# Nine load buffers, and an end that keeps the residual in PSUM, in a mixture-of-experts layer

## The chip, the cores and the metric

The kernel runs on one core of a Trainium2 chip. The metric is the device time of one execution in microseconds (us). The engines are TensorE (PE in the profile), VectorE (DVE), ScalarE (ACT), GpSimd (POOL) and SyncE (SP). SP issues nearly all transfers (DMA); they are carried out by 16 DMA engines. SBUF is the working memory and PSUM the memory that TensorE writes.

## The reference, cut to what matters

One layer of a causal decoder trunk on 256 tokens of 1024 channels, all in float32. It has an RMS norm, an input projection, a pooling mixer and a dilated attention, an output projection added to the residual, and then a mixture of experts, again with an RMS norm, and a last norm:

```
x = x + concat(y_pool, y_attn) @ w_out
t = rmsnorm(x, g_ffn)
logits = t @ w_router + b_router            # 32 experts
top 4 per token, softmax over the four      # combine[token, expert]
for e in range(32):
    gu = t @ w_gu[e] + b_gu[e]              # 1024 x 2048
    gate = min(gu[:, :1024], 7);  lin = clip(gu[:, 1024:], -7, 7)
    act = gate * sigmoid(1.702 * gate) * (lin + 1)
    out += combine[:, e] * (act @ w_down[e] + b_down[e])    # 1024 x 1024
result = rmsnorm(x + out, g_final)
```

Each expert's weights are 8 MB for gate and up and 4 MB for down, so the 32 experts are 402 million bytes that have to be read.

## The kernel before, in words

**Stages.** Up to about 100 us of the profile the kernel runs norm, projections, attention and router. From there it works through the experts, two at a time: a pair is one iteration, and there are 16 pairs. (If an expert has more than 64 tokens the whole set of pairs is run again for the tokens left over; how often is computed on the chip into `further`. For these inputs it is zero.)

**One pair.** Each expert takes up to 64 tokens (`SLOTS`). The tokens of both experts are gathered by matrix products with a 0/1 matrix (`disp`, built by DVE) into xT. For an expert TensorE multiplies xT with gate and up weights (`gu_unit`, eight chunks), ScalarE copies the sum to `gu`, TensorE turns it (`turn_gu`, line 1142), DVE adds the biases (line 840) and clips, ScalarE takes the sigmoid, DVE forms actT, and TensorE multiplies it with the down weights (`down_unit`). ScalarE copies that into ysc. In the next pair TensorE spreads it back to the tokens (`scatter`, two halves of tokens with two halves of columns each) and DVE adds it to the residual acc (line 857). Expert a's down product and gate and up product of the next pair's first expert overlap with the element-wise work of the other one.

**The load buffers.** Weights come in units of 2 MB: four for gate and up, two for down of each expert, 12 for a pair, 192 in all. There are RAW = 8 buffers of 16 KB on each partition. TensorE waits for `raw_loaded` of a buffer, and after the last product with it raises `unit_used`. SP waits for `unit_used` to reach a load's number less RAW, and issues the load (line 322, waiting at 354). SP's queue is worked through in order, whatever an item waits for.

**Before the first pair** SP issues four units of expert 0 and four of expert 1 as soon as their places in SBUF are free, among them b_down into ysc[:, 0] (line 335, after a memset by POOL at line 407), b_gu (line 340) and g_final (gfin, line 342). TensorE runs the gate and up product of expert 0 (line 1155), turns the combine weights (line 1158, `comb_turned`), turns the gate and up biases, 16 transposes (line 1166, `bias_turned`), and starts on the pairs. The first pair has a scatter too: it scatters b_down, weighted with the combine weights that lie in dispT[:, 0].

**The loop** holds two pairs, since 24 units are three times round the eight buffers; the last two pairs are written out behind it.

**The end.** After the last but one unit's product TensorE scatters the pair's first expert (`last_scatter(0)`), then comes the last unit, ScalarE and DVE copy half of its result each (lines 574 and 891), and `last_scatter(1)` adds it. DVE adds the four pieces to acc (line 896). ScalarE squares and sums the rows of each tile of 128 tokens (line 581), DVE takes mean and reciprocal (lines 722 and 723), ScalarE the root (584). POOL multiplies tile 0 with gfin (line 417), DVE tile 1 (line 900), ScalarE and DVE scale one tile each (587, 903), and SP stores them (373).

## Time and profile before

| what | value |
|---|---|
| median of 3 runs | 1038.89 us (1037.91 to 1041.66) |
| the profiled execution | 1037.48 us, its span 1034.8 us |
| PE busy | 956.8 us (92%) |
| DVE, ACT, POOL busy | 28%, 13%, 2% |
| transfers | 419.41 MB, mean 405 GB/s |
| largest groups of transfers | 128 of w_gu and 64 of w_down, 2048 KB each |
| granted clock of TensorE | 0.996 |

The span is from the first to the last instruction of the profiled execution, and the execution's time is 2.7 us more. Engine shares are of the span. In the profile a float32 product of TensorE shows as two MATMUL records and a transpose as one. A row of a timeline that ends with x8 merges eight records. "L909" is line 909, the helper that all matrix products go through, so the tiles tell them apart: raw,xT is gate and up, raw,actT is down, ysc,dispT is a scatter, disp,h a gather. "SPq" is an issue on SP's queue, and "to landing" is the time from it until the semaphore is raised.

### The profile page before, as it was taken

How to read it: one execution, taken by the hardware profiler on the slowest of the kernel's cores; microseconds unless marked ns; L12 is line 12 of the kernel's file. 1: busy time of each engine (PE TensorE's matmuls, PEld its weight loads, DVE VectorE, ACT ScalarE, POOL GpSimd, SP SyncE). 2: the span in 40 equal slices, each digit the busy share in tenths (PEclk: the TensorE clock that was granted, in tenths of full speed). 3: DMA queues.
4: the chain of work that ended last, by engine and by line, in shares of the span. 5: the costliest groups of instructions: out<-in, count | busy, mean ns of one | idle time of the engine just before them, and what ended most of it. 6: DMA issues, size and time to landing. Idle time of an engine off the chain costs nothing.

```text
span 1034.8 us, 12029 instructions
## 1 busy us (share of the span) xinstructions
PE 956.8 (92%) x4841; PEld 427.4 (41%) x4841; DVE 284.8 (28%) x537; ACT 133.7 (13%) x200; POOL 18.2 (2%) x20
## 2 busy tenths in 40 slices
PE   7999999999999989989899999989898999989895
PEld 7988443434343333434243243434343343424331
DVE  6954331222221213122121213113121312213113
ACT  7634001010100000000000000000000000000102
POOL 0500000000000000000000000000000000000000
PEclk9999999999999999999999999999999999999999
DMA  9569899999999999999999999999999999999993
GB/s 359 205 261 396 343 380 415 428 428 430 429 426 429 429 429 428 430 429 426 429 429 429 428 430 429 426 429 429 428 428 430 429 426 429 429 428 428 428 427 146
DMA packets 34489, 419.41 MB, mean 405 GB/s; under 512 B 5300, under 2 KB 5960, under 8 KB 9864
## 3 DMA queue, kind: packets, MB, share of 16 engines
q1 hardware_dynamic: 34432, 419.16, 96.1%
q8 instruction: 13, 0.21, 0.1%
q14 instruction: 4, 0.03, 0.0%
q10 hardware_dynamic: 40, 0.01, 0.0%
HBM read 418.10 MB, written 1.05 MB: 405 GB/s over the span
## 4 chain that ended last, share of the span: by engine, by line
PE 53%; DMA 41%; DVE 4%; issue 1%; ACT 0%; SPq 0%; ACTq 0%; DVEq 0%
PE ps L909 50%; DMA raw<-in_w_down 37%; DMA raw<-in_w_gu 3%; PE ps L1142 2%; DVE woutl L653 1%; DVE xT L750 1%; DMA win<-in_w_in 1%; PE ps L1193 0%; ACT sm L477 0%; PE ps L998 0%; DVE mxs L670 0%; DVE sm L665 0%; PE ps L1166 0%; DVE outs L900 0%; PE ps L1052 0%
## 5 line engine op out<-in xcount | busy, mean ns | idle before, releaser
L909 PE MATMUL ps<-raw,xT 128*64 128x512 f32 x2048 | 459.6, 597 | 23.1 <-DMA raw<-in_w_gu 22.8
L909 PEld LDWEIGHTS ps<-raw,xT 128*64 128x64 f32 x2048 | 140.9, 137 | 322.0 <-issue 265.1
L909 PE MATMUL ps<-raw,actT 128*64 128x512 f32 x1024 | 233.4, 597 | 24.6 <-DMA raw<-in_w_down 24.6
L909 PEld LDWEIGHTS ps<-raw,actT 128*64 128x64 f32 x1024 | 72.2, 136 | 161.2 <-issue 147.4
L840 DVE TENSOR_TENSOR biased<-ps,biasT 128x1024 f32<-128x1024 f32 x32 | 39.2, 1224 | 335.5 <-PE ps L1142 335.5
L541 ACT ACTIVATE gu<-ps 128x1024 f32<-128x1024 f32 x32 | 32.8, 1024 | 527.8 <-PE ps L909 527.8
L857 DVE TENSOR_TENSOR acc<-ps,acc 128x512 f32<-128x512 f32 x64 | 41.2, 686 | 135.4 <-PE ps L909 135.4
L750 DVE TENSOR_TENSOR xT<-ps,gT 128x512 f32<-128x512 f32 x32 | 22.1, 691 | 180.1 <-PE ps L909 180.1
L909 PE MATMUL ps<-ysc,dispT 64*128 64x512 f32 x272 | 67.8, 615 | 0.8 <-DVE ysc L891 0.8
L909 PEld LDWEIGHTS ps<-disp,h 128*128 128x128 f32 x512 | 61.6, 196 | 12.4 <-issue 12.2
L909 PE MATMUL ps<-disp,h 128*128 128x128 f32 x512 | 64.8, 285 | 0.2 <-DVE disp L744 0.2
L546 ACT ACTIVATE sig<-gate 128x512 f32<-128x512 f32 x32 | 20.2, 631 | 272.6 <-DVE gate L843 272.6
L1142 PE MATMUL ps<-cst,gu 128*128 128x128 f32 x256 | 39.7, 299 | 12.9 <-DVE xT L750 12.9
L1142 PEld LDWEIGHTS ps<-cst,gu 128*128 128x128 f32 x256 | 33.5, 211 | 28.7 <-issue 28.7
L909 PEld LDWEIGHTS ps<-ysc,dispT 64*128 64x128 f32 x272 | 24.0, 186 | 44.0 <-issue 29.4
L909 PE MATMUL ps<-hTh,winh 128*128 128x256 f32 x96 | 27.3, 285 | 2.7 <-DVE winl L608 2.7
L909 PE MATMUL ps<-hTl,winh 128*128 128x256 f32 x96 | 27.2, 283 | 0.0
L909 PE MATMUL ps<-hTh,winl 128*128 128x256 f32 x96 | 27.2, 283 | 0.0
L848 DVE TENSOR_TENSOR sig<-gate,sig 128x512 f32<-128x512 f32 x32 | 22.2, 692 | 11.6 <-ACT sig L546 11.6
L551 ACT ACTIVATE ysc<-ps 128x512 f32<-128x512 f32 x31 | 18.5, 597 | 36.6 <-PE ps L909 36.6
L850 DVE SCALAR_TENSOR_TENSOR actT<-lin,sig 128x512 f32<-128x512 f32 x32 | 22.1, 692 | 1.1
L909 PEld LDWEIGHTS ps<-hTh,winh 128*128 128x128 f32 x96 | 18.4, 192 | 2.9 <-issue 2.9
(163 smaller groups left out, 428.6 us busy)
## 6 DMA issues: line engine op xcount, KB each, us to landing
raw<-in_w_gu SPq DMA_DIRECT2D x128, 2048.0 KB, 32.6
raw<-in_w_down SPq DMA_DIRECT2D x64, 2048.0 KB, 34.7
win<-in_w_in SPq DMA_DIRECT2D x16, 512.0 KB, 12.5
wout<-in_w_out SPq DMA_DIRECT2D x4, 1024.0 KB, 9.4
acc<-in_x SPq DMA_DIRECT2D x2, 512.0 KB, 3.8
out<-outs SPq DMA_DIRECT2D x2, 512.0 KB, 3.1
gfin<-in_g_final SPq DMA_DIRECT2D x1, 512.0 KB, 9.5
cst<-in_consts SPq DMA_DIRECT2D x1, 402.0 KB, 7.7
```

The costliest lines, as they stand in the source:

```text
L541: act.activation(gu[:], ps[:, GU[half]:GU[half] + 2, :].rearrange("p a b -> p (a b)"), ACT.Copy).then_inc(gu_copied, 1)
L546: act.activation(sig[:], gate[:], ACT.Sigmoid, scale=ALPHA).then_inc(sig_done, 1)
L551: act.activation(ysc[:, half, :], ps[:, Y[half], :], ACT.Copy).then_inc(outputs_ready, 1)
L653: dve.tensor_tensor(woutl[:, c, :], wout[:, c, :], wouth[:, c, :].bitcast(F32), ALU.subtract).then_inc(wout_low, 1)
L750: dve.tensor_tensor(xT[:, 4 * job:4 * job + 4].rearrange("p c e s -> p c (e s)"), ps[:, M[job], :].rearrange("p (c s) -> p c s", c=4), bc( ...
L840: dve.tensor_tensor(biased[:].rearrange("p m x s -> p (m x) s"), turned, bc(biasT[:, :, bass.ds(e, 1)], P, 2 * DC, SLOTS), ALU.add).then_i ...
L848: dve.tensor_tensor(sig[:], gate[:], sig[:], ALU.mult).then_inc(gsig_done, 1)
L850: dve.scalar_tensor_tensor(out=actT[:, half], in0=lin[:], scalar=1.0, in1=sig[:], op0=ALU.add, op1=ALU.mult).then_inc(act_ready, 1)
L857: dve.tensor_tensor(part, ps[:, M[job % 2], :], part, ALU.add).then_inc(added, 1)
L909: return pe.matmul(out_, lhsT, rhs, start=start, stop=stop, skip_group_check=shared)
L1142: ins = pe.transpose(ps[:, M[m // 4], (m % 4) * P:(m % 4 + 1) * P], gu[:].rearrange("p (u q r) -> p u r q", q=P, r=4)[:, m // 4, m % 4, :] ...
```

## The change

There are nine load buffers, the ninth at 128 KB where xT and gu were, which move to 168 KB; bgu moves to 150 KB and is padded with zeros to 128 partitions, and its 16 transposes become products with the identity over 128 partitions. The ninth load is issued before the pairs, in the place where gfin was; gfin is loaded after the last weights.

The first pair is taken out of the loop and has no scatter. The loop holds three pairs (36 units, four times round nine buffers) and runs four times, and three pairs stand behind it. b_down goes into a tile of its own, bdown, that lies over comb2; the combine weights go to combT; both are multiplied in the scatter of the last pair but one. POOL zeroes bdown after `comb_turned`, and SP waits for that ahead of the pairs' loads.

In the last pair four products with the identity bring the residual into the banks FINAL of PSUM. The last unit is loaded in two pieces of 1 MB with semaphores of their own, and the two halves of `last_scatter(0)` stand between and around its products. The scatters add onto the residual in PSUM. ScalarE squares and sums half tiles out of PSUM and DVE multiplies half tiles out of PSUM with gfin, each in the bank that the other is not in. DVE adds the two half sums of both tiles at once.

In the routing, the cast of the four chosen expert numbers to float (line 733) goes.

```diff
-RAW = 8
-PLACE = (2, 3, 6, 7, 0, 1, 4, 5)
+RAW = 9
...
+ROUND_TRIPLES = (6, 5, 5, 0)
...
-        xT = at("xT", [P, DC, 2, SLOTS], F32, 136 * KB)
-        gu = at("gu", [P, FE], F32, 140 * KB)
+        xT = at("xT", [P, DC, 2, SLOTS], F32, 168 * KB)
+        gu = at("gu", [P, FE], F32, 172 * KB)
...
+        bdown = at("bdown", [P, 512], F32, 182 * KB)
+        combT = at("combT", [P, TT, P], F32, 195 * KB + 256)
...
-        gfin = at("gfin", [P, D], F32, 128 * KB)
-        outs = at("outs", [P, TT, D], F32, 168 * KB)
-        junk3 = [at(f"junk3{t}", [P, D], F32, (184 + 4 * t) * KB) for t in range(TT)]
...
+        bgu = at("bgu", [P, 2 * FE], F32, 150 * KB)
...
+            def load_pieces(e, s):
+
+                rows = w_down[0, bass.ds(e, 1), 4 * P:8 * P, :].rearrange("a (p r) n -> p (a r) n", r=4)
+                for v in range(2):
+                    sp.dma_start(raw[:, PLACE[s], v, :].rearrange("p (r n) -> p r n", r=2),
+                                 rows[:, 2 * v:2 * v + 2, :]).then_inc(piece_loaded[v], 16)
...
-            sp.dma_start(bgu[:], b_gu[0]).then_inc(bgu_loaded, 16)
+            sp.dma_start(bgu[0:E, :], b_gu[0]).then_inc(bgu_loaded, 16)
             sp.wait_ge(logits, 2)
-            sp.dma_start(gfin[:], g_final.rearrange("(a n) -> a n", a=1).broadcast_to([P, D])).then_inc(gfin_loaded, 16)
+            load(0, GU_U, RAW - 1)
             sp.wait_ge(rounds_ready, 1)
...
                     at_ = k - (GU_U if last and k >= 2 * GU_U + DN_U else 0)
-                    sp.wait_ge(unit_used, i * ITER_U + PRE_U + at_ - RAW + 1)
-                    s = buffer(half, at_)
+                    sp.wait_ge(unit_used, i * ITER_U + (PRE_U + at_ - RAW + 1))
+                    s = unit(j, third, at_)[0]
...
+                    elif last and k == ITER_U - 1:
+                        load_pieces(a + 1, s)
...
+            sp.wait_ge(bdown_zeroed, 1)
+            for h in range(2):
+                sp.dma_start(bdown[h * SLOTS:h * SLOTS + E, :], b_down[0, :, h * 512:(h + 1) * 512]).then_inc(bdown_loaded, 16)
+
+            iteration(None, 0, False)
+            with sp.Fori(0, triples) as j:
+                for third in range(3):
+                    iteration(j, third, False)
+            iteration(triples, 0, False)
+            iteration(triples, 1, False)
+            iteration(triples, 2, True)
+            sp.wait_ge(unit_used, number(triples, 2) * ITER_U + PRE_U)
+            sp.dma_start(gfin[:], g_final.rearrange("(a n) -> a n", a=1).broadcast_to([P, D])).then_inc(gfin_loaded, 16)
...
-            pool.wait_ge(rounds_ready, 1)
-            last_pair = pool.snap(pool.value_load(further[0:1, 0:1], min_val=0, max_val=T // SLOTS - 1) * PAIRS + (PAIRS - 1))
-            pool.wait_ge(gfin_loaded, 16)
-            pool.wait_ge(added, last_pair * 4 + 6 + TT)
-            pool.tensor_tensor(outs[:, 0, :], acc[:, 0, :], gfin[:], ALU.mult).then_inc(out_weighted, 1)
+            pool.wait_ge(comb2_zeroed, 1)
+            pool.memset(bgu[E:2 * E, :], 0.0).then_inc(bgu_zeroed, 1)
+            pool.wait_ge(bgu_zeroed, 1)
+            pool.memset(bgu[2 * E:P, :], 0.0).then_inc(bgu_zeroed, 1)
+            pool.wait_ge(bgu_zeroed, 2)
+            pool.wait_ge(comb_turned, 1)
+            pool.memset(bdown[:], 0.0).then_inc(bdown_zeroed, 1)
...
+            iteration(0, False)
+            with act.Fori(1, last_pair) as i:
...
-                act.wait_ge(added, last_pair * 4 + 6 + TT + 2 * t)
-                act.activation(junk3[t][:], acc[:, t, :], ACT.Square, accum_out=ssq[:, t:t + 1]).then_inc(squares, 1)
-            for t in range(TT):
-                act.wait_ge(inv_ready, 4 + t)
-                act.activation(rs[:, t:t + 1], inv[:, t:t + 1], ACT.Sqrt).then_inc(rstd_ready, 1)
+                act.wait_ge(scattered, last_pair * 4 + (2 + 2 * t))
+                for h in range(2):
+                    if h == 1:
+                        act.wait_ge(final_weighted, 2 * t + 1)
+                    act.activation(junk3[:, t, h, :], ps[:, FINAL[t][h], :], ACT.Square,
+                                   accum_out=ssqf[:, t, h:h + 1]).then_inc(final_squared, 1)
+            act.wait_ge(inv_ready, 4)
+            act.activation(rs[:], inv[:], ACT.Sqrt).then_inc(rstd_ready, 1)
             act.wait_ge(rstd_ready, 4)
-            act.wait_ge(out_weighted, 1)
+            act.wait_ge(final_weighted, 2)
             act.activation(outs[:, 0, :], outs[:, 0, :], ACT.Copy, scale=rs[:, 0:1]).then_inc(out_ready[0], 1)
...
-            dve.wait_ge(dispT_zeroed, 1)
-            dve.tensor_copy(dispT[:, 0, :, :], ps[:, 4, 0:T].rearrange("p (t q) -> p t q", t=TT)).then_inc(outputs_ready, 1)
+            dve.tensor_copy(combT[:], ps[:, 4, 0:T].rearrange("p (t q) -> p t q", t=TT)).then_inc(combT_ready, 1)
...
-            with dve.Fori(0, last_pair) as i:
+            iteration(0, False)
...
-            inverse_tile(0, 2 * TT + 1)
-            dve.wait_ge(added, last_pair * 4 + 8 + TT)
-            link(dve.tensor_tensor(outs[:, 1, :], acc[:, 1, :], gfin[:], ALU.mult))
-            inverse_tile(1, 2 * TT + 2)
-            dve.wait_ge(rstd_ready, 5)
+            for t in range(TT):
+                dve.wait_ge(scattered, last_pair * 4 + (2 + 2 * t))
+                for h in (1, 0):
+                    if h == 0:
+                        dve.wait_ge(final_squared, 2 * t + 1)
+                    dve.tensor_tensor(outs[:, t, h * 512:(h + 1) * 512], ps[:, FINAL[t][h], :],
+                                      gfin[:, h * 512:(h + 1) * 512], ALU.mult).then_inc(final_weighted, 1)
+            dve.wait_ge(final_squared, 4)
+            link(dve.tensor_tensor(inv[:], ssqf[:, :, 0], ssqf[:, :, 1], ALU.add))
+            link(dve.tensor_scalar(inv[:], inv[:], 1.0 / D, EPS, ALU.mult, ALU.add))
+            dve.reciprocal(inv[:], inv[:]).then_inc(inv_ready, 1)
+            dve.wait_ge(rstd_ready, 4)
+            dve.wait_ge(final_weighted, 4)
...
-            def scatter(t):
+            def scatter(t, biases):
                 for h in range(2):
                     rows = slice(h * SLOTS, (h + 1) * SLOTS)
+                    if biases:
+                        mm(ps[:, M[h], :], combT[rows, t, :], bdown[rows, :], stop=False)
                     for a in range(2):
-                        ins = mm(ps[:, M[h], :], dispT[rows, a, t, :], ysc[rows, a, :], start=a == 0, stop=a == 1)
+                        ins = mm(ps[:, M[h], :], dispT[rows, a, t, :], ysc[rows, a, :],
+                                 start=a == 0 and not biases, stop=a == 1)
                     ins.then_inc(scattered, 1)
...
                     src = bgu[:, h * FE:(h + 1) * FE].rearrange("e (u q r) -> e u r q", q=P, r=4)[:, m // 4, m % 4, :]
-                    ins = pe.transpose(ps[:, 2, col * E:(col + 1) * E], src, c_("ident", E)[:, 0:E])
+                    ins = mm(ps[:, 2, col * E:(col + 1) * E], src, c_("ident")[:, 0:E], start=col == 0,
+                             stop=col == 2 * DC - 1, shared=True)
             ins.then_inc(bias_turned, 1)
...
+                    if k == 1 and not first:
+                        pe.wait_ge(outputs_ready, i * 2)
+                        if biases:
+                            pe.wait_ge(bdown_loaded, 32)
+                            pe.wait_ge(combT_ready, 1)
+                        scatter(0, biases)
+                    if k == 2 and not first:
+                        pe.wait_ge(added, i * 4 - 4 + (TT + 2))
+                        scatter(1, biases)
                     if k == 3:
-
-                        pe.wait_ge(added, i * 4 + TT + 3)
+                        if not first:
+                            pe.wait_ge(added, i * 4 - 4 + (TT + 3))
                         pe.wait_ge(gated_ready, i + 1)
                         for a in range(2):
                             for t in range(TT):
                                 ins = pe.transpose(ps[:, M[0], (2 * a + t) * P:(2 * a + t + 1) * P],
                                                    gated[:, t, a, :, :].rearrange("p c s -> p (c s)"), c_("ident"))
                         ins.then_inc(disp_turned, 1)
+                    if k == 5 and last:
+                        pe.wait_ge(added, i * 4 - 4 + (TT + 4))
+                        residual_in(0, 0)
+                        residual_in(0, 1)
+                    if k == 6 and last:
+                        residual_in(1, 0)
...
+                if not last:
+                    pe.wait_ge(act_ready, i * 2 + 2)
+                    down_unit(1, 0, *unit(j, third, 10))
+                    pe.wait_ge(gate_clipped, i * 2 + 2)
+                    pe.wait_ge(up_clipped, i * 2 + 2)
+                    turn_gu(i * 2 + 2)
+                    down_unit(1, 1, *unit(j, third, 11))
+                else:
+                    pe.wait_ge(bias_added, i * 2 + 2)
+                    residual_in(1, 1)
+                    pe.wait_ge(act_ready, i * 2 + 2)
+                    down_unit(1, 0, *unit(j, third, 6), Y_LAST)
+                    pe.wait_ge(outputs_ready, i * 2 + 1)
+                    last_scatter(0, 0)
+                    s = unit(j, third, 7)[0]
+                    pe.wait_ge(piece_loaded[0], 16)
+                    down_rows(1, 1, s, (0, 1), Y_LAST)
+                    last_scatter(0, 1)
+                    pe.wait_ge(piece_loaded[1], 16)
+                    down_rows(1, 1, s, (2, 3), Y_LAST).then_inc(unit_used, 1)
+                    pe.wait_ge(outputs_ready, i * 2 + 3)
+                    last_scatter(1, 0)
+                    last_scatter(1, 1)
+
+            def residual_in(t, h):
+                mm(ps[:, FINAL[t][h], :], c_("ident"), acc[:, t, h * 512:(h + 1) * 512], stop=False)
+
+            def last_scatter(a, t):
+                for h in range(2):
+                    rows = slice(h * SLOTS, (h + 1) * SLOTS)
+                    ins = mm(ps[:, FINAL[t][h], :], dispT[rows, a, t, :], ysc[rows, a, :], start=False, stop=a == 1)
+                    if a == 1:
+                        ins.then_inc(scattered, 1)
+
+            iteration(None, 0, False, first=True)
+            with pe.Fori(0, triples) as j:
+                for third in range(3):
+                    iteration(j, third, False)
+            iteration(triples, 0, False)
+            iteration(triples, 1, False, biases=True)
+            iteration(triples, 2, True)
```

## Rows read from the trace of the kernel before

**Rows 1.** The page: rate of transfers in 40 slices, and shares of the chain.
```profile
GB/s 359 205 261 396 343 380 415 428 428 430 429 426 429 429 429 428 430 429 426 429 429 429 428 430 429 426 429 429 428 428 430 429 426 429 429 428 428 428 427 146
...
PE 53%; DMA 41%; DVE 4%; issue 1%; ACT 0%; SPq 0%; ACTq 0%; DVEq 0%
```

**Rows 2.** Chain in order of time: start us, us, what.
```profile
135.37 0.59 PE ps L1193 x4
...
188.98 0.59 PE ps L1193 x4
...
439.78 34.74 DMA raw<-in_w_down
...
498.35 34.91 DMA raw<-in_w_down
...
1013.01 9.18 PE ps L909 x40
```

**Rows 3.** Windows: us, busy of PE, PEld, DVE, ACT, POOL; clock, DMA, GB/s.
```profile
105.00:110.00 5.00, 5.00 (x24) 1.64 (x24) 3.97 (x16) 0.00 (x0) 0.00 (x0) 1.00 0.49 129
...
135.00:140.00 5.00, 5.00 (x26) 1.91 (x26) 2.44 (x10) 0.00 (x0) 0.00 (x0) 1.00 0.71 236
```

**Rows 4.** Timeline of SP's queue: start us, us, the transfers issued.
```profile
71.20 0.80 SPq L335 DMA_DIRECT2D ysc<-in_b_down  x2
...
99.72 0.33 SPq L342 DMA_DIRECT2D gfin<-in_g_final  x1
...
108.78 0.35 SPq L322 DMA_DIRECT2D raw<-in_w_down  x1
...
135.55 0.33 SPq L322 DMA_DIRECT2D raw<-in_w_gu  x1
...
156.22 3.77 SPq L322 DMA_DIRECT2D raw<-in_w_gu  x2
```

**Rows 5.** DMA view, issues at 108.78, 135.55, 159.99: last column us to landing.
```profile
raw<-in_w_down SPq DMA_DIRECT2D x1, 2048.0 KB, 7.7
...
raw<-in_w_gu SPq DMA_DIRECT2D x1, 2048.0 KB, 8.7
...
raw<-in_w_gu SPq DMA_DIRECT2D x1, 2048.0 KB, 11.5
```

**Rows 6.** Line L407 (ns min/median/max), and timeline of PE, 98 to 128 us.
```profile
L407 POOL MEMSET ysc<- x1: 526/526/526, 70.6 to 70.6; 128x512 f32 x1
...
98.64 1.05 PE L909 MATMUL ps<-wrt,h2T 128*128 128x32 f32 x8 [0.61 <-DVE h2T L716]
...
118.75 0.44 PE L1158 MATMUL ps<-cst,comb 128*128 128x128 f32 x2
119.11 2.10 PE L1166 MATMUL ps<-cst,bgu 32*128 32x32 f32 x16
...
127.72 1.99 PE L909 MATMUL ps<-ysc,dispT 64*128 64x512 f32 x8
```

**Rows 7.** Timeline of the end: start us, us, instruction [idle before <-releaser].
```profile
1003.23 3.65 PE L909 MATMUL ps<-raw,actT 128*64 128x512 f32 x16 [0.83 <-DMA raw<-in_w_down]
...
1013.01 3.65 PE L909 MATMUL ps<-raw,actT 128*64 128x512 f32 x16 [1.33 <-DMA raw<-in_w_down]
...
1022.97 1.99 PE L909 MATMUL ps<-ysc,dispT 64*128 64x512 f32 x8 [0.80 <-DVE ysc L891]
...
1024.12 2.48 DVE L896 TENSOR_TENSOR acc<-ps,acc 128x512 f32<-128x512 f32 x4 [1.21 <-PE ps L909]
1025.45 1.06 ACT L581 ACTIVATE junk<-acc 128x1024 f32<-128x1024 f32 x1 [2.64 <-DVE acc L896]
...
1026.41 0.19 ACT L581 ACTIVATION_READ_ACCUMULATOR junk<-acc 128x1 f32 x1
...
1029.46 1.14 ACT L587 ACTIVATE outs<-outs,rs 128x1024 f32<-128x1024 f32 x1
...
1030.37 0.82 SPq L373 DMA_DIRECT2D out<-outs  x2
```

More of the change, by code:

```diff
@@ L75, in constants @@
     put("experts", np.tile(np.arange(E), (P, 1)))
+    put("triples", np.tile(ROUND_TRIPLES, (P, 1)))
     put("limits", np.tile([SLOTS, 2 * SLOTS, 3 * SLOTS, T], (P, 1)))
@@ L217, in hybrid_layer @@
         M = (6, 7)
+        FINAL = ((0, 1), (5, 7))
+        Y_LAST = 6
         def c_(name, rows=P):
@@ L332, in _ @@
             load(1, 1, 5)
-            sp.wait_ge(ysc_zeroed, 1)
-            for h in range(2):
-                sp.dma_start(ysc[h * SLOTS:h * SLOTS + E, 0, :], b_down[0, :, h * 512:(h + 1) * 512]).then_inc(bdown_loaded, 16)
             sp.wait_ge(half_projected, 1)
@@ L1126, in gu_unit, with down_rows @@
                     ins.then_inc(unit_used, 1)
-            def down_unit(half, u, s, value):
-                pe.wait_ge(raw_loaded[s], value)
-                for r in range(4):
+            def down_rows(half, u, s, rows, bank):
+                for r in rows:
                     m = 4 * u + r
```

151 lines of the change are left out of this document (61 added, 90 removed).

## The prediction

> **What bounds the kernel now.** I read the page first. The GB/s line stands at 426 to 430 from the eighth slice to the last but one, and the chain that ended last gives 53% of the span to TensorE (PE) and 41% to DMA [rows 1]. The chain in order of time then shows two stages [rows 2]. In the early pairs of experts it stays on TensorE, and the same four transposes (L1193) come back every 188.98 - 135.37 = 53.6 us. Later it goes through a 35 us w_down load once in each pair, and these loads land at 439.78 + 34.74 = 474.52 and 498.35 + 34.91 = 533.26, so a pair takes 58.74 us. A pair is 12 loads of 2 MB, so one load takes 58.74 / 12 = 4.895 us of the saturated DMA. TensorE needs 53.6 us and has 5.1 us of waiting per pair. The time is therefore set by the stream of 192 loads: when it last stands still, plus 4.895 us for each load after that, plus the tail behind the last but one load. TensorE being faster early on is worth nothing by itself, since it catches up with the stream.
>
> Next I looked for where the stream stands still. The windows show 129 GB/s at 105 to 110 us and 236 GB/s at 135 to 140 us [rows 3]. The issues on SP's queue say why [rows 4]: the first 8 loads are out before gfin, gfin goes out at 99.72, and load 9 only at 108.78, when the first buffer has been used. Load 14 goes out at 135.55, when the sixth unit has been used, which was behind both scatters of the first pair. I number loads in order of use: 1 to 4 are expert 0's gate and up weights, 5 to 8 expert 1's, 9 and 10 expert 0's down weights. Load 9 lands 7.7 us after its issue into an idle queue, at 116.5; load 14 took 8.7 us; load 19 was issued at 156.22 + 3.77 = 159.99 and landed 11.5 us later, at 171.5 [rows 4, 5]. Ten loads at 4.895 would be 48.9 us; 171.5 - 116.5 is 55.0, so 6.1 us of gaps lie between loads 9 and 19. Behind load 19 there are none.
>
> **The stream after the change.** The ninth buffer takes load 9 in place of gfin at 99.7, so it lands by about 112: what was queued before it has drained when the rate collapses, near 107 [rows 3], and 4.9 us follow. Alone this would put the stream one load, 4.9 us, ahead. But SP's queue has another new item: it waits for bdown_zeroed and issues the two b_down transfers before the first pair's loads, load 10 and all that follow. bdown lies over comb2, so POOL zeroes it only after comb_turned, and that comes from the two transposes of L1158, behind the whole first gate/up product: 118.75 + 0.44 = 119.19 [rows 6]. POOL's memset of the same 128x512 shape took 0.53 us, so with two hand-overs 119.75 [rows 6]. The two b_down issues took 0.80 us before [rows 4] and 0.2 us goes to register work: load 10, which needs the first release (the one that let load 9 go at 108.78 before), is issued at about 120.75. Its buffer has then been free for 12 us. POOL's two new memsets of bgu (four times the columns, about 2 us each, starting at 96.6) are over by 101 and cover nothing that waits.
>
> The DMA stands idle from about 112 to 122. Load 10 then meets an idle queue. The bounds are 7.7 us (load 9) and 8.7 us (load 14), the two issues of before that met one [rows 5]; I take 8.0, near load 9, as b_down's 128 KB go just ahead of it and wake the queue: it lands at 128.75. By 119 four releases have come in, so loads 10 to 13 are issued back to back and are 19.6 us of DMA work, to 143.4. Load 14 needs the fifth release. TensorE in the first pair loses two scatters of 1.9 us each [rows 6]; it gains about 1.5 us, since the 16 bias transposes (2.1 us) become 32 fp32 matmul passes of 32 columns (eight of such a form took 1.05 us with the last one's drain, so 32 some 3.6) [rows 6]. So the fifth release comes at about 129.4, 14 us early; the sixth at about 133, the tenth, at 156.2 before [rows 4], near 154, against 167.9, when load 19 would begin. Nothing from load 10 on waits for a buffer. Load 19 lands at 128.75 + 9 x 4.895 = 172.8, against 171.5 before: **+1.3 us** (bounds +1.0 and +2.0 from the 7.7 and the 8.7). So the 10 us hole before load 10 nearly equals what the ninth buffer (4.9) and the vanished later gaps (6.1) give.
>
> The Trainium skill ("DMA: Bandwidth & Descriptors", section "Anatomy of one DMA — SWDGE (gpsimd) path") gives one DMA as about 2.0 us fixed plus bytes at 436 GB/s, for another issuing path than SP's. By that, load 10 would land 6.8 us after its issue and the stream would come out about 0.1 us later than before, not 1.3. The rows here, 7.7 and 8.7, disagree with it, and the sum goes by the rows.
>
> **The loop of three pairs** changes buffer numbers and the code's length; bytes per pair are the same. TensorE has 5.1 us per pair to hide a loop's jump, so I cost it at nothing, and at up to 2 us if one falls into the straight code of the last pairs. The b_down matmuls (four, eight passes of about 0.24 us, 1.9 us) move to the last pair but one and lie in its 5.1 us. The casts of the expert index that go (0.2 us of DVE each) lie beside TensorE's work: 0.
>
> **The last pair.** Four fp32 products bring the residual into PSUM: eight passes at 0.24, 1.9 us. Three stand before the first down product, one before the last but one load's product. TensorE waited 0.83 us and 1.33 us for DMA there [rows 7], 2.2 us together. The cover is thin, and DVE's chain from the turned gate to actT, which also has to be done by 1013, moves by some 0.6 with it: I charge **+0.2 us** (0 to 0.8). After load 191's landing TensorE does the same 16 passes, 8 scatter passes, 16 passes as before: 9.18 us [rows 2]. The two pieces don't shorten this, because TensorE comes to the last load about 4.5 us after load 191 lands and the load is there by then; before, it was not waited for either. gfin is issued behind the pieces, 512 KB, some 1.2 us of transfer, and is needed 12 us after load 191: hidden.
>
> **The tail.** Before [rows 7]: last scatter from 1022.97, first DVE add 1024.12, squares from 1025.45, ScalarE's scaling of its tile from 1029.46 for 1.14, out issues at 1030.37 and 0.41 later. After: the adds go, but both halves of a tile are awaited, so the start is two scatter passes later, 1024.6. ScalarE then squares four half tiles. A whole one took 1.06 plus 0.19 for reading the sum; half is some 0.6 + 0.2, so four take 3.3, to 1027.9. DVE's four products with gfin (0.62 each, as its adds, 2.48 for four) go in the alternate bank meanwhile. Then three small DVE steps (0.55 with their waits), one root 0.25, ScalarE's scaling 1.14: 1029.9, and the issues at 1029.95 and 1030.36 against 1030.37 and 1030.78: **-0.4 us**. Bounds: -1.2, if the halves cost only the 0.53 of pure columns and start at once, and +0.4, if each of the four exchanges between the engines costs 0.2 more.
>
> Sum: +1.3 + 0.2 - 0.4 = **+1.1 us**. The profiled execution took 1037.48 (span 1034.8 and 2.7 around it), so 1038.6; the median of the runs shown is 1.4 above the profiled one, and with that I say 1040.0. About 0.5%, 5.2 us, is what a measurement here can tell from no change.
>
> **Rivals.**
> (a) The gate doesn't hold the loads, for example because comb_turned is passed earlier than I read it. Load 10 then goes out at 108.78 and lands at 116.5, load 13 at 131.2, load 14 (release at 129.4, plus 7.7) at 137.1, load 19 at 161.6: -9.9, with the rest -10.1 us, 1028.8. For it: this is what nine buffers and a first pair without scatter give when unhindered. Against: SP works through its queue in order, and its row at 71.20 [rows 4] is already the pair of b_down issues behind such a memset. 10%.
> (b) The other side, slower: the 10 us hole is not paid back, since the later gaps remain. They are 6.1 us between loads 9 and 19 and come from late releases. It decides if the fifth release comes after about 136 (a bias turn some 6 us longer than before would do it, or the first pair's down product waiting on load 10). Then +1.1 + 6.1 = +7.2, 1046.1. Against: load 10 is needed at about 149 and lands at 128.75. 11%.
> (c) The tail or the last pair is slower than I have it: the exchange of halves and the residual products at their upper bounds, +0.8 and +0.6, and a jump of 2 us: 1043.4. 8%.
>
> **Chances.** Forecast 71%. Faster by over 0.5%: (a) and a little of the forecast's own edge, 0.12. Slower by over 0.5%: (b), and the ends of (c) and of the forecast, 0.14. Same 0.74. The range 1035.0 to 1044.5 holds the forecast and (c).
>
> **What would show it.** SP's first w_down load after the start at 120 to 121.5, directly behind two b_down issues; a hole in GB/s of about 10 us before it and none at 135 to 140; the late landings 1 to 2 us later than 1012.9; out issues about 7 us after the last scatter begins. A load at 108.8 would prove me wrong and (a) right; a second hole after 125 would speak for (b).

## The result and the profile after

| | before | after |
|---|---|---|
| median of 6 runs, us | 1038.98 (1036.90 to 1041.66) | 1043.67 (1041.68 to 1049.11) |
| profiled execution, us | 1037.48 | 1043.27 |
| its span, us | 1034.8 | 1041.5 |

The ratio of after to before is 1.0058, 95% interval 1.0035 to 1.0082: the change makes the kernel slower, by 6.0 us by the ratio and 4.7 by the medians. I had said 1040.0 and "within 0.5%". The time lies in the range, but the kernel has moved by more than its measurement is uncertain, and I had forecast no change. A second set of runs (experiment 1) gives 1.0027 [1.0014, 1.0040], 2.8 us by the ratio, also slower. What follows explains the 6.7 us between the two profiled spans. They lie further apart than the medians: the profiled execution of before is 1.5 us under its median, that of after 0.4 under.

Every kernel has its own line numbers. TensorE's helper, L909 before, is L944 in after, and L939, L942 or L943 in some experiments; SP's load, L322 before, is L335.

The page of after. The rate line and the chain answer to [rows 1]; the line of queue q8 gives packets, MB and share of 16 engines:
```profile
span 1041.5 us, 11985 instructions
...
PEclk9999899999999999999999999999999999999999
...
GB/s 356 205 267 389 189 431 426 426 429 427 427 429 427 429 428 429 429 428 429 429 428 429 428 429 427 429 429 427 430 426 432 425 431 425 429 427 429 429 427 153
...
q8 instruction: 20, 0.33, 0.1%
...
PE 51%; DMA 44%; DVE 3%; ACT 1%; issue 1%; SPq 0%; DVEq 0%; ACTq 0%
```
The fifth slice fell from 343 to 189, and the DMA is saturated from the sixth on, two slices earlier than in [rows 1]. The single 8 in the clock line, absent before, is TensorE at a granted clock of 0.50 from 123.5 to 133.7 us (before had 0.50 from 121.8 to 125.2). The instruction queue carried 13 packets and 0.21 MB before.

SP's queue, answering to [rows 4] (start us, us, transfers issued):
```profile
99.77 0.34 SPq L335 DMA_DIRECT2D raw<-in_w_down  x1
121.28 0.79 SPq L388 DMA_DIRECT2D bdown<-in_b_down  x2
122.11 0.42 SPq L335 DMA_DIRECT2D raw<-in_w_down  x1
122.58 13.11 SPq L335 DMA_DIRECT2D raw<-in_w_gu  x4
```
The windows, answering to [rows 3] (us; busy of PE, PEld, DVE, ACT, POOL; clock, DMA, GB/s):
```profile
110.00:115.00 5.00, 5.00 (x26) 1.67 (x24) 0.61 (x4) 0.00 (x0) 0.00 (x0) 1.00 0.05 16
115.00:120.00 5.00, 5.00 (x26) 1.49 (x22) 0.00 (x0) 0.00 (x0) 0.00 (x0) 1.00 0.00 0
...
125.00:130.00 5.00, 5.00 (x23) 4.66 (x25) 0.82 (x2) 0.00 (x0) 0.00 (x0) 0.50 1.01 433
...
135.00:140.00 5.00, 5.00 (x26) 1.74 (x24) 0.63 (x2) 0.00 (x0) 0.00 (x0) 1.00 1.00 429
```
This is the picture that I had drawn: load 9 goes at 99.77, load 10 stands behind the two b_down issues, the DMA is empty in between, and the second hole of before is gone.

TensorE, 98 to 136 us, answering to [rows 6]:
```profile
99.97 3.47 PE L944 MATMUL ps<-disp,h 128*128 128x128 f32 x16
...
104.19 2.15 PE L944 MATMUL ps<-disp,h 128*128 128x128 f32 x16 [0.16 <-DVE disp L774]
...
120.16 0.44 PE L1199 MATMUL ps<-cst,comb 128*128 128x128 f32 x2
120.44 7.57 PE L944 MATMUL ps<-cst,bgu 128*128 128x32 f32 x32
```
The same gather stands twice: 3.47 us, then 2.15. The granted clock was 0.50 from 99.6 to 103.0 us, so in most of the first one, 1.2 GHz instead of 2.4, and this puts the gate 1.3 us back. And the 16 bias products, 32 records, which I had at 3.6 us, took 7.4 up to the next instruction.

The end, TensorE first and then all engines, answering to [rows 7] (start us, us, instruction, idle before and releaser):
```profile
1004.87 1.99 PE L944 MATMUL ps<-acc,cst 128*128 128x512 f32 x4
1006.78 1.94 PE L944 MATMUL ps<-raw,xT 128*64 128x512 f32 x8
1008.65 1.12 PE L944 MATMUL ps<-acc,cst 128*128 128x512 f32 x2
...
1011.47 3.60 PE L944 MATMUL ps<-raw,actT 128*64 128x512 f32 x16
...
1019.75 1.13 PE L944 MATMUL ps<-acc,cst 128*128 128x512 f32 x2
1020.80 3.65 PE L944 MATMUL ps<-raw,actT 128*64 128x512 f32 x16
...
1031.11 1.99 PE L944 MATMUL ps<-ysc,dispT 64*128 64x512 f32 x8 [0.80 <-DVE ysc L923]
```
```profile
1032.31 0.60 ACT L612 ACTIVATE junk<-ps 128x512 f32<-128x512 f32 x1 [1.36 <-PE ps L944]
1032.31 2.72 DVE L930 TENSOR_TENSOR outs<-ps,gfin 128x512 f32<-128x512 f32 x4 [1.26 <-PE ps L944]
...
1035.91 1.15 ACT L618 ACTIVATE outs<-outs,rs 128x1024 f32<-128x1024 f32 x1
...
1037.08 0.83 SPq L402 DMA_DIRECT2D out<-outs  x2
```
The bracket of a wait for raw is missing on both down products: TensorE waits for no load there any more, which sounds good and is not, since it is now itself late. Next to the scatter (x8 in 1.92 us), the residual's four passes of the same 512 columns also take 1.91 us: 0.48 us a pass, and not 0.24.

Three stretches add up to the span's difference. Landings, here and below, are the trace's own times of the semaphore, to 0.01 us.

| | before, us | after, us | difference | forecast |
|---|---|---|---|---|
| load 191 lands | 1012.88 | 1018.86 | +6.0 | +1.3 |
| last pair, first product to last | 983.55 to 1022.22 = 38.67 | 989.53 to 1030.36 = 40.83 | +2.2 | +0.2 |
| from there to the out issue | 8.15 | 6.72 | -1.4 | -0.4 |

The sum is 6.8 against 6.7 in the spans (TensorE's start in the last pair moved by the same 6.0 as the stream, so the rows don't overlap). And the landings of after show where the stream lost its time:
```
issue    landing   after the one before
122.11   129.93    (load 10)
122.58   134.81    4.89
123.06   139.71    4.89
123.53   146.10    6.39   <- load 13
135.36   151.00    4.91
...
835.24   875.35    4.90
844.88   881.80    6.44   <- load 163
848.32   886.70    4.90
```
Load 19 landed at 175.48, against 171.12 before (its real issue was 159.66; I had taken the end of its row for it, and 171.5 with it). From there both kernels keep 58.73 us a pair to the decimal until load 163 (loads 69 and 81 land at 420.17 and 478.90 in after and at 415.80 and 474.53 in before). So the 6.0 us are: 1.3 forecast, 0.4 of that misreading, 1.2 of load 10 landing at 129.93 and not 128.75, 1.5 at load 13, 1.5 at load 163, and 0.1 left.

### The profile page after: what moved, and what is told of

It reads as the page before. It is cut to its first block, busy times and chain, and to the rows that moved or that the text cites. A ratio compares the mean times of both kernels' runs of the same rounds, so it can differ in the third digit from the quotient of the medians.

```text
span 1041.5 us, 11985 instructions
## 1 busy us (share of the span) xinstructions
PE 969.0 (93%) x4857; PEld 437.7 (42%) x4857; DVE 280.2 (27%) x529; ACT 134.2 (13%) x203; POOL 18.7 (2%) x19
## 4 chain that ended last, share of the span: by engine, by line
PE 51%; DMA 44%; DVE 3%; ACT 1%; issue 1%; SPq 0%; DVEq 0%; ACTq 0%
PE ps L944 48%; DMA raw<-in_w_down 33%; DMA raw<-in_w_gu 11%; PE ps L1180 2%; DVE woutl L684 1%; DVE xT L780 1%; PE ps L1237 0%; ACT sm L503 0%; PE ps L1033 0%; DVE mxs L701 0%; DVE sm L696 0%; DMA cst<-in_consts 0%; PE ps L1087 0%; ACT junk L612 0%; DVE winl L639 0%
## 5 line engine op out<-in xcount | busy, mean ns | idle before, releaser
L944 PE MATMUL ps<-raw,xT 128*64 128x512 f32 x2048 | 460.5, 598 | 22.4 <-DMA raw<-in_w_gu 22.4
L944 PEld LDWEIGHTS ps<-raw,xT 128*64 128x64 f32 x2048 | 141.0, 137 | 322.0 <-issue 265.7
L944 PE MATMUL ps<-raw,actT 128*64 128x512 f32 x1024 | 233.5, 597 | 22.1 <-DMA raw<-in_w_down 22.1
L944 PEld LDWEIGHTS ps<-raw,actT 128*64 128x64 f32 x1024 | 72.7, 136 | 157.7 <-issue 152.6
L887 DVE TENSOR_TENSOR acc<-ps,acc 128x512 f32<-128x512 f32 x60 | 38.9, 687 | 132.7 <-PE ps L944 132.7
L944 PEld LDWEIGHTS ps<-disp,h 128*128 128x128 f32 x512 | 63.0, 200 | 12.4 <-issue 12.2
L944 PE MATMUL ps<-ysc,dispT 64*128 64x512 f32 x256 | 65.8, 614 | 0.8 <-DVE ysc L923 0.8
L944 PE MATMUL ps<-disp,h 128*128 128x128 f32 x512 | 66.2, 288 | 0.2 <-DVE disp L774 0.2
L944 PEld LDWEIGHTS ps<-ysc,dispT 64*128 64x128 f32 x256 | 23.8, 186 | 41.8 <-issue 28.2
L944 PE MATMUL ps<-hTh,winh 128*128 128x256 f32 x96 | 27.3, 285 | 2.1 <-DVE winl L639 2.1
L944 PE MATMUL ps<-hTl,winh 128*128 128x256 f32 x96 | 27.2, 283 | 0.0
L944 PE MATMUL ps<-hTh,winl 128*128 128x256 f32 x96 | 27.2, 283 | 0.0
L944 PEld LDWEIGHTS ps<-hTh,winh 128*128 128x128 f32 x96 | 18.4, 192 | 2.3 <-issue 2.3
```

The source lines that it names most:

```text
L887: dve.tensor_tensor(part, ps[:, M[job % 2], :], part, ALU.add).then_inc(added, 1)
L944: return pe.matmul(out_, lhsT, rhs, start=start, stop=stop, skip_group_check=shared)
```

## The experiments

Nine kernels ran beside the kernel before. Each ratio is to the kernel before as it ran beside that experiment. The cuts of code show the edit where it matters; what isn't shown is the kernel named.

**1. The changed kernel again.**

> The changed kernel unchanged, for a second profile beside the others. Theory A (the gate): SP's first load of the pairs goes out at 120 to 123 us again and the landing of the load that starts the last pair is 5 to 6 us later than the 983.5 of before; the exact issue follows whether TensorE's clock is at half speed in the first gather. Theory B (the later jumps of 1.8 and 1.6 us in the landings, at load 13 and at load 164, are a fixed cost of the larger code): both jumps stand at the same loads again. If B is wrong they are at other places or gone. Time ratio 1.004 to 1.008.

Measured: 1043.45 us, ratio 1.0027 [1.0014, 1.0040], span 1042.0. The two jumps are there again, at the same loads (load 13 at 146.38 and load 163, which the expectation calls 164, at 882.21, 6.19 and 6.35 us after the one before), so they belong to the program. This time the gather ran at the full clock. Its start-up was 2.05 us later altogether (load 7 issued at 89.97 against 87.92) and load 10 was issued at 122.60: from the same start that is 120.55, and my 120.75 was right for the full clock. The half clock in the gather is a matter of the execution.

**2. The gate out of SP's way.** Wait and b_down issues behind the first pair's loads:
```
-            sp.wait_ge(bdown_zeroed, 1)
-            (two b_down issues)
             iteration(None, 0, False)
+            sp.wait_ge(bdown_zeroed, 1)
+            (two b_down issues)
```


> SP's wait for bdown_zeroed and the two b_down issues stand behind the first pair's loads instead of ahead of them; b_down is used only in the last pair but one. Theory A: load 10 goes out at about 110 (first release) instead of 122.1 and lands at about 118; no hole of 11 us is left; the later landings come 9 to 11 us earlier than in the changed kernel (some 4 to 5 us earlier than before), and the time is 10 us lower than the changed kernel's: about 1033. Rival (the hole is paid back by the gaps in any case, and it is the end and the code that cost the 5 us): less than 3 us lower.

Measured: 1037.67 us, ratio 0.9970 [0.9956, 0.9984], span 1038.1: 5.8 us less than the changed kernel (experiment 1), but only 3.1 less than before, where rival (a) of the prediction had 10.1. Load 10 is issued at 112.26 (its release is used at once) and lands at 120.27, 9.7 us before that of after. But TensorE and SP show what then comes late (timeline of TensorE, and of SP's queue, and three windows):
```profile
122.72 7.57 PE L943 MATMUL ps<-cst,bgu 128*128 128x32 f32 x32
130.11 1.95 PE L1179 MATMUL ps<-cst,gu 128*128 128x128 f32 x8
```
```profile
115.69 22.35 SPq L335 DMA_DIRECT2D raw<-in_w_gu  x4
```
```profile
125.00:130.00 5.00, 5.00 (x23) 5.00 (x24) 0.00 (x0) 0.00 (x0) 0.00 (x0) 0.59 1.00 429
130.00:135.00 5.00, 5.00 (x18) 2.66 (x19) 3.13 (x5) 0.63 (x1) 0.00 (x0) 0.50 0.72 308
135.00:140.00 5.00, 5.00 (x22) 1.50 (x20) 0.93 (x2) 0.00 (x0) 0.00 (x0) 0.89 0.31 66
```
The four issues in one row stretch over 22 us: the fourth, load 14, waits for the fifth release until 137.72 and lands 10.52 us after load 13. The fifth release is behind the 7.4 us of bias products and a slow stretch at clock 0.50, from 125.9 to 136.1. This is the mechanism of rival (b). In after the fifth release is nearly as late (load 14 is issued at 135.36, not near 129.4), but the gate has put load 13 off until 146.10, so nothing stands still.

**3. The 16 bias transposes of before in place of the 16 products**, on top of 2:
```
-            pool.memset(bgu[E:2 * E, :], 0.0) ...        (and the second one)
-                    ins = mm(ps[:, 2, col * E:(col + 1) * E], src, c_("ident")[:, 0:E], ...)
+                    ins = pe.transpose(ps[:, 2, col * E:(col + 1) * E], src, c_("ident", E)[:, 0:E])
```


> The kernel with the gate moved, and the 16 bias transposes of before in place of the 16 products over 128 partitions (POOL's two memsets of bgu go with them). Theory A: those products take 7.4 us of TensorE against 2.0, and with the gate moved they hold back the fifth release, so that the stream stands still for some 5 us from 133 us on. With the transposes the fifth release comes 5 to 8 us earlier, the hole shrinks to under 1 us, and the landings after it are 4 to 6 us earlier than with the gate moved alone; time 4 to 6 us lower, about 1033. Rival (the fifth release is late for TensorE's half clock, which comes in any case): 0 to 2 us lower.

Measured: 1032.36 us, ratio 0.9934 [0.9909, 0.9958], span 1031.2. Timeline of TensorE, and of SP's queue:
```profile
101.60 2.13 PE L939 MATMUL ps<-disp,h 128*128 128x128 f32 x16
...
120.82 2.10 PE L1202 MATMUL ps<-cst,bgu 32*128 32x32 f32 x16
...
124.55 8.50 PE L939 MATMUL ps<-raw,xT 128*64 128x512 f32 x32 [0.47 <-issue]
```
```profile
113.69 16.29 SPq L335 DMA_DIRECT2D raw<-in_w_gu  x4
```
The transposes take 2.0 us up to the next instruction, the fifth release comes at 129.66, and the hole at load 14 is gone: load 10 lands 6.30 us after load 9, 1.4 more than usual, and loads 11 to 19 land 4.88 to 4.95 apart. Load 191 lands at 1008.63, 6.9 us ahead of experiment 2. The clock isn't the full one here either: it was 0.50 from 124.0 to 127.4 us, which is why 32 records that take 7.09 us elsewhere take 8.50 in the last row. But that is 3.4 us at half clock and not 10.2. Of the 8.1 us by which the fifth release is earlier than in experiment 2, 5.4 are the shorter bias work and 0.5 an earlier start (load 7 issued at 89.77 against 90.25); the 2.2 left I put down to the clock in experiment 2, 1.4 of it in the first gather (3.58 us against 2.13). So the rival of the expectation, the half clock, has a share, and the bias form the larger one.

Another thing shows in the landings. b_down, 128 KB, is now issued behind load 21 (L389 on SP's queue at 160.94), and its 64 packets of 2 KB move at 170.7 to 174.6 us, in the full stream. Loads 21 and 22 land 1.1 us late together. The same two loads are 0.9 to 1.1 us late in all four kernels with b_down there (experiments 2, 3, 4 and 8), and in none of the others; by its bytes it would be 0.3 us (an estimate, 128 KB at 429 GB/s).

**4. The early ninth load alone**, experiment 3 with `sp.wait_ge(unit_used, 1)` ahead of load 9.

> The kernel with the gate moved and the bias transposes, but the ninth load is issued only when the first buffer has been used, as in the kernel before; the ninth buffer stays. Theory A (the ninth buffer is worth one load that goes into the hole before the first release, 4.9 us less what later waits take back): load 9 lands at about 118 instead of 112.8, load 10 at about 123 instead of 119.1; nothing later stands still for a release, so all landings stay 4 us later; time 3.5 to 4.5 us higher than with the early issue, about 1036. Rival (the depth of nine loads is what counts, not the early one): 0 to 1 us higher.

Measured: 1037.05 us, ratio 0.9973 [0.9957, 0.9988], span 1035.4. Load 9 is issued at 110.50 instead of 101.58, and 4.2 us of span are lost, near one load of 4.9. So the ninth buffer is worth its one load, as the prediction had it, once nothing stands behind it.

**5. The gate alone, in the kernel before:** `sp.wait_ge(comb_turned, 1)` ahead of the pairs' loads.

> The kernel before with one thing more: SP waits for comb_turned ahead of the pairs' loads. Theory A (what a gate costs is its delay less what the later gaps give back): load 9 goes out at 119.3 instead of 108.8, and lands at 127 instead of 116.5; loads 13 to 19 lose most of their 6.1 us of gaps, so load 19 lands 4 to 6 us later than 171.5 and the time is 4 to 6 us higher than before. Rival (the forecast's own rival b, gaps stay): 10.5 us higher. Rival (hidden): under 2 us.

Measured: 1044.86 us, ratio 1.0043 [1.0027, 1.0059], span 1041.3. SP's queue:
```profile
99.68 0.33 SPq L342 DMA_DIRECT2D gfin<-in_g_final  x1
119.57 0.97 SPq L322 DMA_DIRECT2D raw<-in_w_down  x2
```
Load 9 lands at 127.38 instead of 116.50, 10.9 us later, and load 191 at 1019.46, 6.6 later: 4.3 us came back from the later gaps. The idea of a hole that is partly paid back holds. Nearly all of the +6.5 in the span is this. With its holes closed this kernel, still with loops of two pairs, has a jump too: load 12 lands 5.72 us after load 11, 0.8 more than usual, with an instruction packet at 140.3 us. Before has that packet at 139.9, in a hole.

**6. Without the residual products**, after as it is; the output lacks the residual, and the first scatter into each bank starts it afresh:
```
             def residual_in(t, h):
-                mm(ps[:, FINAL[t][h], :], c_("ident"), acc[:, t, h * 512:(h + 1) * 512], stop=False)
+                pass
```


> The four products that bring the residual into PSUM are left out, so the output lacks the residual; all else as in the changed kernel. Theory A (each of these fp32 products over the full 128x128 array takes 0.96 us, not the 0.48 that the forecast gave it, and 3.8 us are more than the 2.2 us of waiting in the last pair): TensorE waits for DMA again ahead of the down products of the last pair, and the stretch from the first product of the last pair to the last one is 38.7 to 39.0 us as before, against 40.8; time 1.5 to 2.2 us lower. Rival (the stretch is longer because the scatter is split and the loads land late): 0 to 0.5 us lower.

Measured: 1040.75 us, ratio 1.0010 [0.9995, 1.0026], span 1038.1. Timeline of TensorE:
```profile
1007.61 3.65 PE L944 MATMUL ps<-raw,actT 128*64 128x512 f32 x16 [0.84 <-DMA raw<-in_w_down]
...
1017.42 3.65 PE L944 MATMUL ps<-raw,actT 128*64 128x512 f32 x16 [1.35 <-DMA raw<-in_w_down]
...
1027.72 1.99 PE L944 MATMUL ps<-ysc,dispT 64*128 64x512 f32 x8 [0.80 <-DVE ysc L923]
```
Both waits of [rows 7] are back, with 0.84 and 1.35 us (0.83 and 1.33 before), and the last pair takes 39.0 us instead of 40.8. 3.8 us of products against 2.2 us of waits leave 1.6 uncovered, and the last pair is 1.8 us shorter without them: that is most of the last pair's loss of 2.2. The other 0.4, also in this kernel (39.0 against 38.7), I didn't take apart.

**7. The whole end of before on after:** one last load, DVE adds, norm from the sum in SBUF, no residual products.

> The changed kernel with the end of before: no residual products, the last unit in one load, adds by DVE, norm out of SBUF, POOL's product. Theory A: the last pair is 2.2 us shorter (40.8 to 38.7), the tail behind the last down product 1.4 us longer, so the time is 0.5 to 1.0 us lower than the changed kernel's and the end was no gain. Rival (the new end gains what its tail gains): 1.4 us higher.

Measured: 1042.32 us, ratio 1.0030 [1.0018, 1.0043], the ratio of experiment 1; span 1040.7. The last pair takes 38.7 us and the tail to the out issue 8.4, 47.1 in all, against 40.8 + 6.7 = 47.6 in after. New end and old end cost about the same; the 0.5 to 1.0 us that I expected can't be told from nothing by these intervals.

**8. Residual of the first tile before the last pair**, on top of 3. Two of the four products go ahead of the pair's first product, where TensorE waits for the stream anyway, and the first tile's scatter adds onto them, so two DVE additions go:
```
+                if last:
+                    residual_in(0, 0)
+                    residual_in(0, 1)
...
+                        ins = mm(ps[:, banks[h], :], dispT[rows, a, t, :], ysc[rows, a, :], start=False, stop=False)
```


> The kernel with the transposes, and the residual of the first 128 tokens brought into PSUM ahead of the last pair's first product, where TensorE waits for a load; the scatter of the pair before goes onto it, and DVE's two adds of it fall away. Theory A (last pair bound by TensorE through 3.8 us of residual products, 1.9 us not covered): the last pair is 1.5 to 2.1 us shorter, time as much lower than with the transposes alone. Rival (DMA sets the end of the last pair): 0 to 0.5 us lower.

Measured: 1030.29 us, ratio 0.9916 [0.9894, 0.9938], span 1029.4. Timeline of TensorE:
```profile
977.63 1.98 PE L939 MATMUL ps<-acc,cst 128*128 128x512 f32 x4
979.55 3.65 PE L939 MATMUL ps<-raw,xT 128*64 128x512 f32 x16
...
996.61 1.12 PE L939 MATMUL ps<-acc,cst 128*128 128x512 f32 x2
```
The last pair takes 38.8 us (979.55 to 1018.3) and keeps the shorter tail. In experiment 3 TensorE waited 1.24 us for a load at 979.30; now it works there. This version beats before by 8.7 us by its ratio, and after by more.

**9. Before with TensorE's loop over four pairs instead of two.** Bytes and work stay the same; only the loop's code is longer:
```
-            with pe.Fori(0, last_two) as j:
-                iteration(j, 0, False)
-                iteration(j, 1, False)
-            iteration(last_two, 0, False)
-            iteration(last_two, 1, True)
+            with pe.Fori(0, fours) as j:
+                for q in range(4):
+                    iteration(j, q, False)
+            for q in range(3):
+                iteration(fours, q, False)
+            iteration(fours, 3, True)
```


> The kernel before, with TensorE's loop over four pairs instead of two; nothing else. Theory B (an instruction packet of 16 KB holds back one DMA engine by about 1.1 us, the packets go round eight places, and a later landing shows only for the first packet after the last hole in the stream, and for the ninth, the seventeenth): there are more q8 packets in the saturated stream than the six of before; one more jump of 1.4 to 1.6 us between two landings for every eight of them, and none elsewhere; time 1.5 us higher with 9 to 16 packets, more if the loop is fetched again in each turn. Rival C (jumps belong to the issue of loads, not to packets): no jump, time within 0.5 us of before. Rival D (TensorE itself stalls at the loop's jump): gaps of TensorE, no jump in the landings.

Measured: 1044.89 us, ratio 1.0055 [1.0035, 1.0075], span 1044.2 (in this profiled execution 3.4 us come from elsewhere, below). The page of this kernel, and its DMA view of 528.5 to 529.5 us:
```profile
q8 instruction: 42, 0.69, 0.3%
```
```profile
q1 hardware_dynamic: 35, 0.48, 111.8%
q8 instruction: 1, 0.02, 6.6%
```
42 packets instead of 13, so the loop's code is fetched anew in each turn, ten packets a turn (with loops of two and of three pairs there are none between 216 or 320 us and the last pairs). One packet of 0.69 MB / 42 = 16 KB holds 6.6% of 16 engines for 1 us: one engine of the 16 for 1.06 us. Behind the start-up the landings are 4.8 to 5.0 us apart but for four places (packets counted from the one at 142.8 us, during load 14, where this kernel has a hole as before has):
```
9th packet, 342.3 us:    347.39   6.45 after the one before
17th packet, 529.1 us:   534.80   6.37
25th packet, 707.5 us:   712.60   6.45
33rd packet, 931.7 us:   934.29   6.37
```
Each jump is some 1.5 us, and no later landing gives any of it back; together 6.1 us. These four loads had been issued 27 to 37 us before they landed, so no late release made the jumps. Load 191 lands 9.5 us later than before; 1.6 of this is a later start-up and 1.8 later releases (TensorE again had a stretch at clock 0.50, near 125 us). TensorE stops for the fetches too, but only where the loop jumps back. Timeline of TensorE:
```profile
345.02 5.35 PE L909 MATMUL ps<-raw,xT 128*64 128x512 f32 x16 [2.76 <-issue]
...
580.37 5.35 PE L909 MATMUL ps<-raw,xT 128*64 128x512 f32 x16 [2.72 <-issue]
```
The load for the first row had landed at 340.94, so all 2.76 us are the jump's; the load for the second landed at 578.84, which leaves 1.5 us. Behind both the clock was at 0.50 for 3.4 us. This is what the prediction had in mind, and TensorE makes it up in its waits of 5.1 us a pair: no landing moved with it.

## Why the prediction was wrong, point by point

**What failed: fetches of instructions, put at nothing in two terms.** The one is "Load 19 lands at 128.75 + 9 x 4.895", which gives the stream no loss behind load 10. The other is the loop of three pairs at "nothing, and at up to 2 us if one falls into the straight code of the last pairs". I looked for the cost of longer code on TensorE, where 5.1 us per pair would hide it, and it is on the DMA, which is the bound. After carries 20 instruction packets. At 143.5 us comes the first since the hole, where the stream jumps by 1.5 us (load 13), and at 879.2 the ninth, the first of the straight code, where it jumps by 1.5 (load 163). Before has seven packets in the saturated part (140, 163, 192, 216, 939, 959, 994 us), fewer than a ninth, and its first two fell beside its two holes, during load 14 (8.7 us to landing) and load 18 (10.0 us). What they cost there can't be read apart from the late releases; loads that met an idle queue took 7.7 to 8.0 us, so some of the 6.1 us of gaps that I put down to releases may be theirs. The jump at load 13 isn't due to longer code, then: before fetches at that place too, and the change closed the hole beside it, as experiment 5 does with the loop of two pairs. Only the jump at load 163 is the loop's.

Experiment 9 shows the cause by itself: more packets, nothing else, and jumps at the 9th, 17th, 25th and 33rd alone. Which of the 16 DMA engines a packet falls on is in no view; that they take turns over half of them, and that the first and ninth meet the one that is last with each load, is inferred from the count. Two things stay open. One is why a packet that holds an engine for 1.1 us costs the stream 1.5. The other is that in experiments 3 and 8 the 7th and 15th packets of the program (141 and 874 us) cost 0.4 us or less, and the 8th and 16th (166 and 894 us) 1.0 to 1.2, where in the other kernels with this loop the 7th and 15th cost 1.2 to 1.7. The distance of eight holds in both, the place doesn't.

The Trainium skill ("Runtime: NRT & Kernel Launch", section "Instruction fetch mechanics") has blocks of 16 KiB, fetched by the sequencer's own DMA queue, at a cost that is mostly hidden, and a stall for a fetch where a branch leaves a window of two of them; it gives TensorE a memory of 128 KiB, which is eight. The trace agrees on the size (16 KB) and on the stall (2.8 us at 342.3 in experiment 9). It doesn't agree on a window of two: a loop of three pairs, seven to eight packets by the ten of four pairs (an estimate), isn't fetched again, and that of four pairs is, which fits the eight. And for a stream that has no slack the cost isn't hidden (6.1 us in experiment 9).

**The residual products: "eight passes at 0.24, 1.9 us".** They take 0.48 us a pass at 512 columns, 3.8 us, and TensorE had 2.2 us of waits to hide them. The 0.24 came from products with 64 rows or 64 columns of the array, of which two run side by side: in after, records of raw,xT start in twos, 7 ns apart, and the next two 0.43 us later, which is also the step from one full-tile record to the next. The row to take stood in the same trace in the gather's full 128*128 tiles (as here at 104.19: 16 passes of 128 columns in 2.1 us, 0.13 each, and four times that for 512 columns). The upper bound of 0.8 was too low by the same error; experiments 6 and 8 confirm both the price and its remedy. The last pair cost +2.2, not +0.2.

**The gate: right in place, 1.2 us late in time.** SP, b_down, load 10 and the idle DMA of about 10 us are as described (121.28, 122.11, and 0 GB/s at 115 to 120). Load 10 took 7.8 us to landing, between my two bounds. The formula of the Trainium skill ("DMA: Bandwidth & Descriptors", section "Anatomy of one DMA — SWDGE (gpsimd) path") gives an estimate of 6.8, and the trace doesn't agree with it. My upper bound, 8.7, wasn't an idle queue: load 14 of before was issued at 135.55 and load 13 landed at 136.07. What I had not priced is a gather at clock 0.50 (3.47 us against 2.13), which experiment 1 shows to be absent from other executions.

**The bias products: "32 some 3.6".** They are 16 products in 32 records, and took 7.38 us up to the next instruction in all five kernels that have them (after and experiments 1, 2, 6 and 7), with a record every 0.233 us. In after the clock fell to 0.50 in the middle of them, at 123.5, and the step stayed 0.233: they aren't bound by TensorE's clock. Lines of L944 in after, 104.1 to 120.4 us, and of the tile bgu (ns min/median/max):
```profile
L944 PEld LDWEIGHTS ps<-disp,h x16: 195/196/197, 104.2 to 106.0; 128*128 128x128 f32 x16
```
```profile
L944 PEld LDWEIGHTS ps<-cst,bgu x32: 308/330/330, 120.3 to 127.5; 128*128 128x128 f32 x32
L944 PE MATMUL ps<-cst,bgu x32: 313/421/421, 120.4 to 127.6; 128*128 128x32 f32 x32
```
Each record comes with a load of a whole 128x128 stationary tile, a column of bgu out of four (q, r=4 in the code), and I read the 7.4 / 32 = 0.23 us a record as set by this load and not by the 32 columns that I had counted. That the stride is why it takes 330 ns and not 196 was not tried. In after the gate hides this. But it is the larger part of why rival (a)'s -10.1 was wrong for a kernel without the gate: experiment 2 is 3.1 us under before, and with the transposes too it is 6.9 (0.66% of 1039).

**The payback: right.** The ninth load's early issue is worth 4.2 us (experiment 4), the later gaps 4.3 (experiment 5; I had 6.1), and nothing behind load 10 waits for a buffer. **The tail: better than forecast**, -1.4 against -0.4. Both engines start 1.2 us after the scatter's first pass, not 1.6, and the four squares overlap their sum reads: 2.7 us for the four and not 3.3.

In the spans the stream's term and the loop's together missed by 4.7 (3.0 of it from instruction packets, 1.2 from load 10, most of that the gather at half clock), the last pair's by 2.0, and the tail gave 1.0 back. So the sum was +1.1 and the spans show +6.7. Without the half clock, which comes and goes, it would still have been some +5.5 (an estimate, 6.7 less 1.2). That the range still held the time is due to rival (c)'s jump of 2 us, not to the working.

## What to carry to other kernels

When the bound is a saturated DMA stream, everything that adds a transfer to it counts, the fetches of TensorE's code too: look at the instruction queue's packets and at the spacing of landings, and keep a loop short enough that it is not fetched again in each turn. When a change closes a hole in the stream, the fetches beside it stand in the full stream from then on. One more buffer buys one load only if SP's queue has nothing in front of the next load that waits for a late result; put such waits behind the loads. For a new matmul take the price from a row with the same tile of the array, and count work that is added where TensorE waits for DMA against that wait: four products behind it cost 1.8 us (experiment 6), and two of them moved ahead of it gave as much back (experiment 8).

## What the runs showed of the hardware that I had not expected

- A 16 KB packet of instructions holds one DMA engine for about 1.1 us, and in experiment 9 every eighth one delays all landings after it by about 1.5 us (four jumps of 6.4 to 6.5 us instead of 4.9).
- 128 KB of b_down in 64 packets of 2 KB cost the saturated stream 0.9 to 1.1 us in four kernels, about three times what its bytes would take at 429 GB/s.
- Products of full 128*128 fp32 tiles take 0.96 us for 512 columns (two records of 0.48), those of 128*64 or 64*128 tiles half of that, 16 records in 3.6 us, since two start 7 to 13 ns apart and run side by side.
- The weight load of bgu took 330 ns, that of h 196, both 128x128 fp32. With 32 of the former in a row (7.4 us) the granted clock fell to 0.50 within them, for 10.2 us in after and in experiment 2 and 6.9 us in experiments 1, 6 and 7. With the 16 transposes (2.0 us) it fell too, 0.7 us behind them in before, for 3.4 us in before and in experiments 3, 4, 5 and 8, and for 6.9 in experiment 9.
- Two loads of 1 MB in place of one of 2 MB cost the stream nothing: they land 2.47 and 2.45 us apart, 4.92 together.
